# Two hybrid decoder layers: expert activations in 4x4 blocks, gate rows per token on VectorE, differences on GpSimd

## What is computed

```python
s = jnp.einsum('thpd,hpnd->thpn', q, sub_keys)
sv, si = lax.top_k(s, K)                       # 16 of 128, for both halves of the key
cand = (sv[:, :, 0, :, None] + sv[:, :, 1, None, :]).reshape(T, H, K * K)
best, pos = lax.top_k(cand, K)                 # 16 pairs (i, j) for each token and head
eidx = jnp.take_along_axis(cidx, pos, axis=-1) # expert = 128 i + j
gate = jax.nn.softmax(best, axis=-1)
def chunk(args):
    a = jnp.einsum('chkd,cd->chk', expert_u[ec], xc)
    w = gc * jax.nn.gelu(a, approximate=False)
    return jnp.einsum('chk,chkd->cd', w, expert_v[ec])
```

## Time and profile before

| | us |
|---|---|
| median of 3 runs | 2413.84 (2411.94 to 2419.11) |
| profiled execution, span from first to last instruction | 2416.4 |
| gate stage, first layer | 721 to 849 |
| DMA | 353.44 MB, 146 GB/s over the span |

### The profile page before, as it was taken

How to read it: one execution, slowest core, us unless ns; L and a number is a source line. 1 busy time by engine, 2 the same in 40 slices (tenths; PEclk the granted TensorE clock), 3 DMA queues, 4 the chain that set the end, 5 groups by cost and what they waited for, 6 DMA issues and landing times.

```text
span 2416.4 us, 43624 instructions
## 1 busy us (share of the span) xinstructions
PE 2251.2 (93%) x14328; PEld 1980.3 (82%) x14328; DVE 1599.0 (66%) x2831; ACT 1207.0 (50%) x2154; POOL 30.9 (1%) x48
## 2 busy tenths in 40 slices
PE   6989989999998899999988998999999988999997
PEld 6877789999985578788777867999999855887886
DVE  5646657777779955555557456477777799555555
ACT  4435444544457744444444344445545676454553
POOL 1000000000000000000000000000000000000000
PEclk9989999999999999999989899999999999999999
DMA  3611435555540045555545114455555300555554
GB/s 141 229 63 67 147 123 182 182 182 182 181 158 0 0 162 194 195 196 192 174 142 201 54 54 155 141 182 182 182 182 183 130 0 0 192 193 197 192 196 141
DMA packets 96307, 353.44 MB, mean 146 GB/s; under 512 B 11056, under 2 KB 11088, under 8 KB 95856
## 3 DMA queue, kind: packets, MB, share of 16 engines
q1 hardware_dynamic: 94032, 341.90, 42.0%
q0 software_dynamic: 2208, 10.66, 1.2%
HBM read 351.47 MB, written 1.05 MB: 146 GB/s over the span
## 4 chain that ended last, share of the span: by engine, by line
PE 58%; issue 28%; DVE 8%; DMA 2%; ACT 2%; DVEq 1%; POOL 1%; SPq 0%; POOLq 0%; ACTq 0%
PE wide L1210 13%; PE acc L1199 13%; PE acc L1200 13%; PE acc L1201 13%; DVE big L1137 4%; DVE hot_j L1124 1%; DMA raw<-in_front 1%; PE wide L1385 1%; PE tr L1310 1%; PE acc L1338 1%; POOL rstd L410 0%; DVE lo L699 0%; PE acc L1433 0%; PE acc L1356 0%; DVEq L1122 0%
## 5 line engine op out<-in xcount | busy, mean ns | idle before, releaser
L699 DVE TENSOR_TENSOR lo<-raw,hi 128x1024 fp32r<-128x1024 f32 x648 | 792.4, 1224 | 587.0 <-ACT hi L445 582.1
L445 ACT ACTIVATE hi<-raw 128x1024 fp32r<-128x1024 f32 x648 | 686.7, 1060 | 519.5 <-DMA raw<-in_peer_v 357.3
L1199 PE MATMUL acc<-xT_hi,lo 128*128 128x256 f32 x2560 | 733.6, 287 | 8.9 <-DVE xT_lo L780 7.3
L1200 PE MATMUL acc<-xT_lo,hi 128*128 128x256 f32 x2560 | 731.4, 286 | 0.0
L1201 PE MATMUL acc<-xT_hi,hi 128*128 128x256 f32 x2560 | 731.0, 286 | 0.0
L1199 PEld LDWEIGHTS acc<-xT_hi,lo 128*128 128x128 f32 x2560 | 498.9, 195 | 11.8 <-issue 9.8
L1200 PEld LDWEIGHTS acc<-xT_lo,hi 128*128 128x128 f32 x2560 | 499.0, 195 | 0.2
L1201 PEld LDWEIGHTS acc<-xT_hi,hi 128*128 128x128 f32 x2560 | 498.7, 195 | 0.0
L1210 PE MATMUL wide<-hi,w_lo 128*128 128x512 f32 x1024 | 319.0, 393 | 12.8 <-DVE w_lo L1158 12.8
L1210 PE MATMUL wide<-hi,w_hi 128*128 128x512 f32 x1024 | 318.7, 393 | 0.0
L1210 PE MATMUL wide<-lo,w_hi 128*128 128x512 f32 x1024 | 318.0, 392 | 0.0
(11 more groups left out here) (241 smaller groups left out, 1824.4 us busy)
## 6 DMA issues: line engine op xcount, KB each, us to landing
raw<-in_peer_u SPq DMA_DIRECT2D x256, 512.0 KB, 3.2
raw<-in_peer_v SPq DMA_DIRECT2D x256, 512.0 KB, 3.2
raw<-in_front SPq DMA_DIRECT2D x136, 512.0 KB, 3.3
ln_par<-in_ln POOLq DMA_DIRECT2D x10, 512.0 KB, 5.4
w<-in_cmp_w POOLq DMA_DIRECT2D x2, 2048.0 KB, 10.0
xs<-in_x SPq DMA_DIRECT2D x2, 512.0 KB, 7.0
keys<-in_sub_keys POOLq DMA_DIRECT2D x2, 512.0 KB, 4.3
out<-xs SPq DMA_DIRECT2D x1, 1024.0 KB, 3.9
```

The source lines that it names most:

```text
L445: nc.scalar.activation(hi[:, s], raw[:, s], ACT.Identity).then_inc(hi_done, 1)
L699: nc.vector.tensor_tensor(lo[:, s], raw[:, s], hi[:, s].bitcast(F32), ALU.subtract).then_inc(lo_done, 1)
L1199: mm(dst, lo[:, s, c], xh[:, k], start=k == 0, stop=False)
L1200: mm(dst, hi[:, s, c], xl[:, k], start=False, stop=False)
```

## The change

`big` gets another layout: blocks of four experts by four tokens, `[128, 32, 64, 4, 4]` for (j / 4, token / 4, j % 4, token % 4). Four tokens of one tile are 16 bytes in a row, the 4x4 block is 64. ScalarE's Gelu writes it so, and the splits before the V products read it so. The scratch rows of the search get a name of their own (`scr`) at the same place.

In the gate stage the differences i - place are one GpSimd instruction per group, 512 values from `iota` and `picksT`. ScalarE then takes Abs and Relu(1 - d), each over the whole group, for all groups. `gated_rows` becomes four VectorE instructions, one per token, with the token's place and gate as per-partition scalars. The two bf16 products of TensorE, their four constant tensors and the 0/1 rows on VectorE go.

```diff
-        big = at("big", [P, NKEYS, SEQ], F32, 0)
+        big = at("big", [P, NKEYS // JB, SEQ // TB, JB, TB], F32, 0)
...
+                pool.wait_ge(tr_read[X_PK % 2], OPEN + l * (NTR // 2) + NTR // 2)
+                pool.sem_inc(apart, 1)
+                with pool.Fori(0, NG // HOTS) as i:
+                    for e in range(HOTS):
+                        pool.wait_ge(acc_ready, l * NREADY + (R_G + 1 - HOTS) + (i * HOTS + e))
+                        toks = picksT[:, 0, bass.ds(i * (4 * HOTS) + 4 * e, 4)].unsqueeze(2).broadcast_to([P, 4, P])
+                        nc.gpsimd.tensor_tensor(hot_i[:, e], iota[:].unsqueeze(1).broadcast_to([P, 4, P]), toks,
+                                                ALU.subtract).then_inc(differences_ready, 1)
...
-                    nc.scalar.activation(big[:, i * 8 + e], acc[:, e % 2, :SEQ], ACT.Gelu).then_inc(acc_read[e % 2], 1)
+                    nc.scalar.activation(big[:, i * 2 + e // JB, :, e % JB], acc[:, e % 2, :SEQ].rearrange("p (g t) -> p g t", t=TB),
+                                         ACT.Gelu).then_inc(acc_read[e % 2], 1)
...
-                    act.wait_ge(acc_ready, l * NREADY + (R_G + 1 - HOTS) + (i * HOTS + e))
-                    for r in range(4):
-                        tok = i * (4 * HOTS) + (4 * e + r)
-                        ins = nc.scalar.activation(hot_i[:, e % HOTS, r], iota[:], ACT.Abs,
-                                                   bias=picksT[:, 0, bass.ds(tok, 1)], scale=-1.0)
-                    ins.then_inc(distance_done, 1)
+                    act.wait_ge(differences_ready, l * NG + (i * HOTS + (e + 1)))
+                    nc.scalar.activation(hot_i[:, e], hot_i[:, e], ACT.Abs).then_inc(distance_done, 1)
...
-                    if e % 2 == 1:
-
-                        return
...
-                    dve.wait_ge(apart_j_ready, l * NG + (i * HOTS + (e + 1)))
-
-                    nc.vector.scalar_tensor_tensor(
-                        out=hot_j[:, e % HOTS], in0=wide[:, e % HOTS // 2, 512 * (e % 2):512 * (e % 2) + 512].rearrange("p (t j) -> p t j", t=4),
-                        scalar=0.0, in1=picksT[:, 2, bass.ds(i * (4 * HOTS) + 4 * e, 4)].unsqueeze(2).broadcast_to([P, 4, P]),
-                        op0=ALU.is_equal, op1=ALU.mult).then_inc(hot_j_ready, 1)
-
-                def one_hot(i, e):
-
-                    dve.wait_ge(distance_done, l * NG + (i * HOTS + (e + 1)))
-                    nc.vector.tensor_scalar(hot_i[:, e], hot_i[:, e], 0.0, None, ALU.is_equal).then_inc(hot_i_odd, 1)
+                    for r in range(4):
+                        tok = i * (4 * HOTS) + (4 * e + r)
+                        ins = nc.vector.tensor_scalar(hot_j[:, e % HOTS, r], iota[:], picksT[:, 1, bass.ds(tok, 1)],
+                                                      picksT[:, 2, bass.ds(tok, 1)], ALU.is_equal, ALU.mult)
+                    ins.then_inc(hot_j_ready, 1)
...
-                    part = big[:, :, bass.ds(i * (4 * HOTS) + 4 * e, 4)].rearrange("p j t -> p t j")
-                    nc.vector.tensor_tensor(part, acc[:, e % 2].rearrange("p (t j) -> p t j", t=4), part,
+                    part = big[:, :, bass.ds(i * HOTS + e, 1)].rearrange("p a g j t -> p (a g) j t")
+                    nc.vector.tensor_tensor(part, acc[:, e % 2].rearrange("p (t a j) -> p a j t", t=TB, j=JB), part,
                                             ALU.mult).then_inc(acc_read[e % 2], 1)
...
-                    for e in range(HOTS):
-                        gates_of(i, e)
-                        if nxt is not None:
-                            apart_j(*nxt, e)
...
+                with pe_.Fori(0, NG // HOTS) as i:
                     for e in range(HOTS):
                         gates_of(i, e)
```

More of the change, by code:

```diff
@@ L106 @@
 HOTS = 4
+JB, TB = 4, 4
 X_XT, X_Q, X_K, X_NQ, X_KT, X_CD, X_PC, X_AT, X_XT2, X_PK = 0, 4, 8, 12, 16, 18, 20, 24, 42, 46
@@ L621, in _ @@
                     act.wait_ge(acc_ready, l * NREADY + R_SCR + i + 1)
-                    nc.scalar.activation(big[:, S0 + 4 * c:S0 + 4 * c + 4, p * P:(p + 1) * P],
+                    nc.scalar.activation(scr[:, 4 * c:4 * c + 4, p * P:(p + 1) * P],
                                          acc[:, p].rearrange("p (u n) -> p u n", u=4),
@@ L670, in _ @@
                     for e in range(HOTS):
-                        distances(i, e + 1)
+                        if e + 1 < HOTS:
+                            distances(i, e + 1)
+                        else:
+                            distances(i + 1, 0)
                         one_hot(i, e)
@@ L676, in _, with split_w_hi @@
                     one_hot(NG // HOTS - 1, e)
-                def split_w_hi(j, s):
-                    nc.scalar.activation(w_hi[:, s], big[:, j], ACT.Identity).then_inc(w_hi_done, 1)
+                def split_w_hi(i, c, s):
+                    nc.scalar.activation(w_hi[:, s].rearrange("p (g t) -> p g t", t=TB), big[:, i + c // JB, :, c % JB],
+                                         ACT.Identity).then_inc(w_hi_done, 1)
                 for b in range(2):
@@ L1512, in _ @@
                 transpose_heads(X_PK + 1, [picks[:, 2, tt] for tt in range(TT)], P)
-                pe_.wait_ge(whole_ready, 3 + l + 1)
-                for b in range(TT):
-                    pe_.wait_ge(wide_read[b], OPEN + l * NWIDE + W_V)
-                def apart_j(tt, i, e):
-                    dst = wide[:, e // 2, 512 * (e % 2):512 * (e % 2) + 512].rearrange("p (t j) -> p t j", t=4)
-                    mm(dst, places_b[:, tt], ident_b[:, bass.ds(i * (4 * HOTS) + 4 * e, 4)].unsqueeze(2).broadcast_to([P, 4, P]),
-                       start=True, stop=False)
-                    mm(dst, ones_b[0:1], minus_iota[0:1].unsqueeze(1).broadcast_to([1, 4, P]),
-                       start=False, stop=True).then_inc(apart_j_ready, 1)
                 def gates_of(i, e):
                     pe_.wait_ge(acc_read[e % 2], OPEN + l * (NACC // 2) + (i * 2 + (A_G + e) // 2))
-                    if e % 2 == 0:
-                        pe_.wait_ge(hot_i_ready, l * (NG // 2) + (i * 2 + (e // 2 + 1)))
-                    else:
-                        pe_.wait_ge(hot_i_odd, l * (NG // 2) + (i * 2 + (e // 2 + 1)))
+                    pe_.wait_ge(hot_i_ready, l * NG + (i * HOTS + (e + 1)))
                     pe_.wait_ge(hot_j_ready, l * NG + (i * HOTS + (e + 1)))
@@ L1537, in gates_of @@
                     ins.then_inc(acc_ready, 1)
-                def step(i, nxt):
+                with pe_.Fori(0, NG // HOTS) as i:
                     for e in range(HOTS):
                         gates_of(i, e)
-                        if nxt is not None:
-                            apart_j(*nxt, e)
-                half = NG // HOTS // TT
-                for e in range(HOTS):
-                    apart_j(0, 0, e)
-                with pe_.Fori(0, half - 1) as i:
-                    step(i, (0, i + 1))
-                step(half - 1, (1, 0))
-                with pe_.Fori(half, 2 * half - 1) as i:
-                    step(i, (1, i - (half - 1)))
-                step(2 * half - 1, None)
                 wide_free(l, W_V)
```

42 lines of the change are left out of this document (14 added, 28 removed).

## The result

The changed kernel takes **2433.97 us** (median of 4 runs, 2429.28 to 2436.84), the kernel before 2414.94 beside it: 1.0065 times as long, 95% interval 1.0044 to 1.0086. That is +19 us, where +15 was forecast. The profiled execution has a span of 2427.6 against 2416.4.

A forecast was written before the change was run, and what follows sets the result against it. VectorE was taken to bound the gate stage at 1.97 us a group. 128 groups by 2.12 less 1.97 give +19, less 4 for the ends +15: 2429 us, own range 2405 to 2465, over all cases 2345 to 2470.

The forecast's parts named there:

- The time and the sign: Whole kernel: slower by 15 us, at 2429 us, with a gate-stage group at 2.12 us instead of 1.97.
- The multiplication: VectorE in the gate stage: 0.75 us of queue per group in the new layout, between 0.60 and 1.19.
- Rival D: Gate stage: stepping PSUM stream costs as much as the old layout, group 1.98, 2410 to 2415 us; chance 0.10.
- The rows: VectorE's gated rows in the gate stage: four instructions per group cost 0.92 us together, between 0.79 and 1.04.
- B: Gate stage: VectorE's own sum alone sets the pace, 1.67 us a group, 2372 us; chance 0.32.
- The subtraction: GpSimd in the gate stage: one instruction over 512 values per group takes 1.05 us, between 0.87 and 1.21.
- ScalarE: Gate stage: two steps over 512 values, 633 ns for Abs and 707 for Relu, below every other sum.
- Exclusion: Gate stage: GpSimd's subtraction never runs beside VectorE's rows, so 1.05 + 0.92 + 0.15 for handing over make 2.12 us.
- The layout's gain: Gate stage: the multiplication is hidden beside the subtraction at any price up to 1.05 us, so its saving isn't seen.
- rival C: Gate stage: TensorE falls to its lower clock without the bf16 products, group 2.33 us, 2456 us; chance 0.08.
- The ends: Start and end of the gate stage: earlier first product and shorter last multiplication save 2 us per layer, 4 in all.
- The other stages: Stages around the gates: 16-byte runs for ScalarE and VectorE stay hidden behind TensorE, costing nothing.

The follow-up runs named there:

- 6: Changed kernel plus two unread bf16 products per group on TensorE: 2417.0 us, 1.0001 of the kernel before.
- 8: Changed kernel plus two unread bf16 products per group, and GpSimd's subtraction also waiting for the previous group's gated rows: 2426.8 us, 1.0037 of the kernel before.
- 9: Changed kernel with GpSimd's subtraction also waiting for the third of the previous group's four row instructions: 2397.24 us, 0.9914 of the kernel before.
- experiment 3: Changed kernel without GpSimd's subtraction, ScalarE taking Abs of the bare row of numbers: 2364.19 us, 0.9775 of the kernel before.
- Experiment 4: Changed kernel with the four row instructions reading a copy of iota in PSUM, subtraction kept: 2401.52 us, 0.993 of the kernel before.
- experiment 2: Changed kernel with the old layout of big: 2515.49 us, 1.0401 of the kernel before.
- 7: Changed kernel with the old layout and two unread bf16 products per group on TensorE: 2459.89 us, 1.0175 of the kernel before.

## Why the prediction was right, and where it wasn't

- **The time and the sign** were right (+19 against +15; a group 2.09 against 2.12), by a mechanism that was half right. That the group came so near is in part luck: hardly a group takes 2.12, 2.09 is the mean of groups of 1.75 and of some 2.37, and experiments 6, 8 and 9 make 2.00, 2.06 and 1.80 of the same instructions.
- **The multiplication** was priced at 0.75 between 0.60 and 1.19. It is 0.60: the PSUM stream in steps of 512 bytes costs nothing (677 ns against 685 dense). Rival D falls with that, and so does what the Trainium skill's page "Advanced Engine Details and Errata", section "Memory Cachelines", would have made of it, carried over to VectorE.
- **The rows** were priced at 0.92 for four. Undisturbed they last 1.11 to 1.15 and take 1.02 of the queue: 1.62 with the multiplication (experiment 3), where 1.67 was predicted for B. The two errors nearly cancelled.
- **The subtraction** was 1.05, measured 1.04. **ScalarE** was 633 and 707, measured 630 and 706.
- **Exclusion** is the step that failed in its form. The prediction added 1.05 + 0.92 + 0.15 as if the two never overlapped. Experiment 4 shows that they exclude each other only where the rows' input is in SBUF; but only about 0.78 of the subtraction counts, and only what falls behind the multiplication. Group times of 1.80 to 2.09 come from the same instructions (experiments 9, 8 and 6, and the changed kernel itself), by when the subtraction starts. A fixed 2.12 can't give these. The sign it named, one row instruction in four of about a microsecond, came out at 77 of 512, since the wait is often shorter and 20 groups of 63 hardly have one. The Trainium skill's page "SBUF — State Buffer", section "Who interferes with whom", has the lock last a whole instruction; the traces show it for a part of one (1.12 for a lead of 0.77, where the subtraction still runs 0.27 us into the rows).
- **The layout's gain is not hidden**, against what the prediction said: experiment 2 is 81 us slower than the changed kernel, and with TensorE kept busy it is still 43 (7 against 6).
- **The clock** was set as rival C, in which TensorE becomes the bound. In the changed kernel it never does, but the clock falls to 0.84 and that costs 17 us through the start of the subtraction (6). A partial C was in the result.
- **The ends** were put at −4 in all and came out at about +3. The four subtractions in a row ahead of the loop hold up VectorE, the effect that the prediction had only inside the loop.
- **The other stages** were put at nothing, and a time that changes outside the stage was named as a sign of being wrong. In the one pair of traces the output products are 7.5 us shorter, by the clock as far as the estimate above goes: higher in their first ten microseconds, and without one short fall that other kernels with the change do have. Price of the layout there: Gelu's write is 383 to 384 ns as before, the split 401 after 400, so that term was right.
- **What decides B** was put as subtraction, rows and hand-over below 1.97 together. It is rather the lead: at 0.65 a group takes 1.80 where the kernel before took 1.97.

## What to carry to other kernels

When GpSimd works beside VectorE, look not at the sum of their times but at which of VectorE's instructions each GpSimd start falls on: put it beside one that reads PSUM, and tie its start to that instruction if another engine's end would otherwise set it. Measure each part of a change that does two things alone; here the layout alone gained 44 us and the rest alone lost 98, and together they lost 19, since on top of the rest the layout is worth 81. And where products are taken off an engine, look at its clock and at who starts on its next end.

## What was not expected of the hardware

- GpSimd's 512-value subtraction (1.04 us) stops VectorE's 128x128 rows with an SBUF input for about 0.78 us from its start, one row up to 1.2 us instead of 0.33; the same rows with their input in PSUM (0.41) run beside it undisturbed, and so does the two-input multiplication with one operand in PSUM (0.69 against 0.70 without any subtraction). Why 0.78 and not 1.04 stays open.
- Which of the two waits isn't fixed. The durations of the subtractions and of the row instructions of the changed kernel, least, median and most in ns:

```profile
L436 POOL TENSOR_TENSOR hot_i<-iota,picksT x128: 1034/1040/2016, 718.2 to 2054.5; 128x512 f32<-128x512 f32 x128
```

```profile
L1121 DVE TENSOR_SCALAR hot_j<-iota,picksT x512: 327/334/1217, 722.2 to 2059.3; 128x128 f32<-128x128 f32 x171
```

  In the loop it is VectorE, and the subtraction takes at most 1.17. The subtractions of 2.02 us are the third of the four in a row ahead of the loop, beside VectorE's split with two SBUF inputs, which is stretched itself (2.06 instead of 1.21); and in the earlier trace rows GpSimd waited.
- Both streams in SBUF in steps of 1024 bytes cost 0.60 us for 512 values; in 64-byte pieces they cost nothing, with PSUM stepping 512 bytes in return.
- Two unread bf16 products in TensorE's pauses made a kernel 17 us faster, or 56.
